# One ring of 22 places for all expert weights, loaded two slabs at a time over buffers that lie idle

## The chip, the core and the metric

The kernel runs on one core of a Trainium2 chip. The metric is the device time of one execution in microseconds (us), as the median of several runs; a profiled execution gives the trace. TensorE does the matmuls, VectorE (DVE in the rows) and ScalarE (ACT) the elementwise work, and SyncE (SP) does nothing but issue DMAs, which bring the weights from device memory into the on-chip memory. All engines run their own instruction streams and meet at semaphores.

## The reference

One inference step of a two-layer decoder for 288 tokens (256 of a prompt and 8 x 4 new ones), in fp32, width 1024. Each layer mixes three recurrent branches (retention, gated linear attention, RWKV-7) and then applies a feed-forward part. The change concerns the second layer, whose feed-forward part picks two of eight experts for each token:

```python
def swiglu(h, w1, w3, w2):
    return (jax.nn.silu(h @ w1) * (h @ w3)) @ w2

def moe_swiglu(h, router, w1, w3, w2):
    logits = (h @ router).astype(jnp.float32)
    top_v, top_i = lax.top_k(logits, TOP_K)
    probs = jax.nn.softmax(top_v, axis=-1)
    gate = jnp.sum(jax.nn.one_hot(top_i, N_EXPERTS, dtype=jnp.float32) * probs[..., None], axis=-2)
    out = jnp.zeros(h.shape, jnp.float32)
    for e in range(N_EXPERTS):
        out = out + gate[..., e:e + 1] * swiglu(h, w1[e], w3[e], w2[e]).astype(jnp.float32)
    return out.astype(h.dtype)
```

w1 and w3 of an expert are 1024 x 2816, w2 is 2816 x 1024; the three are 34.6 MB in fp32, for each of eight experts.

## The kernel before

The program runs through both layers in stages; in the second layer the mixing stage ends with a merging stage (`mix_out`: three pairs of gate slabs, four of the RWKV branch and four of the output projection, eleven "join pairs" in all), and then comes `experts`. Weights arrive as slabs of 128 x 1024 fp32 (512 KB) on a ring of eight places, `ring`, in the order in which TensorE uses them. SP issues one DMA for a slab as soon as the slab that held the place before is done, which it reads from one counter, `slab_done`.

In `experts` the tokens of an expert are gathered and the expert runs over at most `cap` of them. There are eight passes here, the experts in order of the number of their tokens: two passes at a capacity of 88, two at 80, two at 76 and the rest, two here, at 72. For each capacity there is one piece of code, and a loop runs it twice. A pass has

- an up part: 44 slabs of w1 and w3, one after the other by turns, each 16 matmul calls (8 blocks of rows by two halves of 64 columns), with ScalarE's silu and VectorE's product behind it;
- between: the matrix that scatters the results (`scatter_matrix`) and the gather for the next pass (`gather_tokens`);
- a down part: eight column blocks of w2, two at a time (`down`, 44 matmul calls each), then the results are added to the tokens (`add_up`, `to_tokens`).

TensorE's code for the up part is a loop (`pe.Fori`) of five turns over eight slabs and four slabs behind it, that of the down part a loop of four turns over two column blocks. The up slabs use the eight places of `ring`; the down weights come as 24 slabs (16 of 512 KB, 8 of 384 KB) on six places of their own over `proj`, an idle buffer. At the start of the first pass eight up and six down slabs have been asked for. SP's order in a pass is: six down slabs, up slabs 8 to 43, the first eight up slabs of the expert that follows, the other 18 down slabs. In the last pass the expert that follows is none, and its eight slabs are loaded and not used.

These lines of the profile belong to it: L302 matmuls of the earlier stages, L455 matmuls of an up slab, L2659 of a down slab, L2618 and L2624 the gather, L2646 the scatter matrix, L2670 and L2677 the additions, L2704 the sums of the closing norm; L442, L2524 and L2530 are SP's loads.

Of the kernel before, what the change touches and what calls it, by code (L numbers as in the profile page):

```python
# [22 lines left out]
D = 1024  # L23
# [4 lines left out]
T = NP + NS  # L28
# [26 lines left out]
RING = 8  # L55
SIDE_BEGUN = 6
# [39 lines left out]
FF_SLABS = UP_SLABS + DOWN_SLABS  # L96

# [124 lines left out]
def build(nc, xT_in, w_mix, w_lora, w_rank, w_gkup, vec_in, vecf_in, router_in, w_ff, s_ret, s_gla, s_rw,  # L222
# [133 lines left out]
    slab_done = nc.alloc_semaphore(name="slab_done")  # L356
    rank_in = [nc.alloc_semaphore(name=f"rank_in{s}") for s in range(2)]
# [1752 lines left out]
    def slab_width(j):  # L2110
        return 6 if j >= UP_SLABS and (j - UP_SLABS) % 3 == 2 else KT

# [12 lines left out]
    def mix_out(nc, block, sig, layer, delta, joined):  # L2125
# [32 lines left out]
        def _(sp):  # L2158
            load_group(sp, S_RW_OUT, 1)
            load_first_group(sp, S_OUT)  # L2160
            if dense:
                for j in range(FF_SLABS):
# [298 lines left out]
    def experts(nc, block, sig, layer, merge, rs):  # L2461
# [22 lines left out]
        down_ring = proj[:, :, :].rearrange("p n t -> p (n t)")[:, 0:6 * D].rearrange("p (s k n) -> p s k n", s=6, k=KT)  # L2484
        DRING = 6
        down_in = [sig(f"down_in{s}") for s in range(DRING)]
# [4 lines left out]
        FREED = 4, 5, 6, 7, 0, 1, 2, 3  # L2491
# [16 lines left out]
        def _(sp):  # L2508
            def freed_up(p, n):

                if n >= RING:
                    return count(p, FF_SLABS, FF0 + n - RING + 1)
                return count(p, FF_SLABS, FF0 - FF_SLABS + max(range(n, UP_SLABS, RING)) + 1)

            def load_up(p, e, n):
                load_ff_slab(sp, e, n, n % RING, freed_up(p, n))

            def load_down(p, e, d):
                if d >= DRING:
                    sp.wait_ge(slab_done, count(p, FF_SLABS, FF0 + UP_SLABS + d - DRING + 1))  # L2520
                else:
                    sp.wait_ge(slab_done, count(p, FF_SLABS, FF0 - DRING + d + 1))
                n = slab_width(UP_SLABS + d)
                sp.dma_start(down_ring[:, d % DRING, 0:n], w_ff[e, UP_SLABS + d, :, 0:n]).then_inc(down_in[d % DRING], 16)  # L2524

            def load_following(i, e, turn):
                for n in FREED:
                    sp.wait_ge(slab_done, freed_up((i, turn), n))
                    settle(sp)
                    sp.dma_start(ring[:, n], w_ff[e, n]).then_inc(slab_in[n], 16)  # L2530

            def expert_of(i):
                return sp.value_load(ctl[0:1, i], min_val=0, max_val=NE)
# [33 lines left out]
        def _(pe):  # L2567
# [111 lines left out]
            def expert(p, cap):  # L2679
# [634 lines left out]
```

## Time and profile before

| what | us |
| --- | --- |
| median of 3 runs | 2499.25 (2497.41 to 2500.42) |
| the profiled execution: its time | 2499.8 |
| the profiled execution: span of its trace | 2498.0 |
| TensorE matmuls busy | 2434.0 (97% of the span) |
| TensorE weight loads busy | 2026.7 (81%) |
| VectorE busy | 1287.7 (52%) |
| ScalarE busy | 606.7 (24%) |

The span goes from the first to the last instruction of the trace; 1.8 us of the execution lie outside it. The granted TensorE clock was 0.997 of full speed over the execution. An engine's busy time says nothing about what it waits for in a given stage: the matmul row is counted as busy from the start of a matmul to a modelled end, so a stream that waits a little at every slab still looks busy.

### The profile page before, as it was taken

To read this page: it belongs to the slowest core of one execution; us is meant where nothing else is said; L and a number is where in the kernel's file an instruction comes from. 1 tells how busy PE (TensorE), PEld (TensorE's weight loads), DVE (VectorE), ACT (ScalarE), POOL (GpSimd) and SP (SyncE) were. 2 spreads that over 40 slices of the span, in tenths; PEclk is the share of its full clock that TensorE was granted. 3 is DMA by queue.
4 is the path that set the end of the run, shared out by engine and by line. 5 is a ranking of instruction groups with operands and counts; after the bars stand their busy time and mean duration, and the time that the engine had idled before them with its cause. 6 is when DMAs were issued, how large, how long until landed. Compare 5 with 4: busy or idle time off the path is not lost. (4 is left out here: it accounts for less than half of the span.)

```text
span 2498.0 us, 104094 instructions
## 1 busy us (share of the span) xinstructions
PE 2434.0 (97%) x45930; PEld 2026.7 (81%) x45930; DVE 1287.7 (52%) x3333; ACT 606.7 (24%) x1798; POOL 0.2 (0%) x4
## 2 busy tenths in 40 slices
PE   9999999999999999999999999999999999999998
PEld 8987666666698999898766666669899989888887
DVE  7666666666686675756666566668311111111111
ACT  2233333433311100223332334331111111111111
POOL 0000000000000000000000000000000000000000
PEclk9999999999999999999999999999999999999999
DMA  6334432222243453423443222223799999999997
GB/s 250 112 137 162 148 137 88 83 84 80 92 153 128 153 179 127 142 106 139 164 161 127 85 77 84 84 105 145 297 356 398 380 376 409 396 379 402 395 390 308
DMA packets 146064, 500.46 MB, mean 200 GB/s; under 512 B 18784, under 2 KB 23520, under 8 KB 143360
## 3 DMA queue, kind: packets, MB, share of 16 engines
q1 hardware_dynamic: 145792, 496.44, 53.6%
q8 instruction: 219, 3.59, 0.6%
q14 instruction: 53, 0.43, 0.1%
HBM read 476.08 MB, written 20.29 MB: 199 GB/s over the span
## 5 line engine op out<-in xcount | busy, mean ns | idle before, releaser
L302 PE MATMUL psum<-hT,ring 128*64 128x144 f32 (+1 forms) x4568 | 457.1, 346 | 3.4 <-DVE hT L2422 1.7
L455 PE MATMUL psum<-work,ring 128*64 128x88 f32 (+3 forms) x11264 | 417.5, 232 | 15.4 <-DMA ring<-w_ff_dram 5.7
L455 PEld LDWEIGHTS psum<-work,ring 128*64 128x64 f32 x11264 | 399.2, 136 | 34.6 <-issue 29.6
L302 PEld LDWEIGHTS psum<-hT,ring 128*64 128x64 f32 x4568 | 291.8, 137 | 97.0 <-issue 11.7
L2958 DVE TENSOR_TENSOR work<-psum,work 128x88 f32<-128x88 f32 (+3 forms) x176 | 42.4, 241 | 361.8 <-PE psum L455 361.6
L2659 PE MATMUL psum<-work,proj 128*64 128x88 f32 (+3 forms) x5632 | 204.8, 232 | 6.8 <-issue 5.6
L2659 PEld LDWEIGHTS psum<-work,proj 128*64 128x64 f32 x5632 | 197.5, 136 | 14.0 <-issue 11.5
L1768 ACT ACTIVATE work<-psum 128x256 f32<-128x256 f32 (+4 forms) x320 | 103.9, 362 | 349.9 <-PE psum L1679 84.8
L302 PE MATMUL psum<-y_ret,work 128*64 128x144 f32 x2400 | 157.8, 288 | 0.8 <-DVE y_ret L532 0.8
L302 PE MATMUL psum<-work 128*64 128x144 f32 (+4 forms) x2096 | 154.1, 282 | 4.3 <-DVE work L1259 3.6
L302 PEld LDWEIGHTS psum<-y_ret,work 128*64 128x64 f32 x2400 | 150.2, 138 | 1.3 <-issue 1.3
L302 PEld LDWEIGHTS psum<-work 128*64 128x64 f32 (+2 forms) x2096 | 121.3, 136 | 30.7 <-issue 11.3
L2949 DVE TENSOR_TENSOR xT<-xT,psum 128x288 f32<-128x288 f32 x64 | 29.1, 454 | 220.6 <-PE psum L2670 219.6
L2743 ACT ACTIVATE work<-psum 128x88 f32<-128x88 f32 (+3 forms) x176 | 41.7, 237 | 376.7 <-PE psum L455 373.2
L302 PE MATMUL psum<-y_ret,ring 128*64 128x144 f32 (+1 forms) x1280 | 126.8, 332 | 2.5 <-ACT work L1768 2.5
L302 PEld LDWEIGHTS psum<-y_ret,ring 128*64 128x64 f32 x1280 | 79.5, 137 | 18.5 <-ACT work L1768 4.5
L324 PE MATMUL psum<-hT,ring 128*128 128x288 f32 x252 | 72.8, 408 | 0.0
L1564 PEld LDWEIGHTS psum<-work 64*64 64x64 f32 x1408 | 47.3, 134 | 29.4 <-issue 17.7
L547 DVE TENSOR_TENSOR y_gla<-psum,y_gla 128x288 f32<-128x288 f32 x72 | 33.0, 458 | 73.2 <-PE psum L302 72.6
L302 PE MATMUL psum<-hT,work 128*64 128x144 f32 x928 | 68.8, 287 | 0.0
L2747 ACT ACTIVATE work<-psum 128x88 f32<-128x88 f32 (+3 forms) x64 | 15.2, 237 | 218.3 <-PE psum L2659 218.3
L519 DVE TENSOR_TENSOR work<-ring 128x512 f32<-128x512 f32 (+1 forms) x90 | 54.7, 608 | 19.0 <-PE psum L302 19.0
(518 smaller groups left out, 3723.9 us busy)
## 6 DMA issues: line engine op xcount, KB each, us to landing
ring<-w_ff_dram SPq DMA_DIRECT2D x424, 512.0 KB, 7.6
ring<-w_mix_dram SPq DMA_DIRECT2D x256, 512.0 KB, 4.2
proj<-w_ff_dram SPq DMA_DIRECT2D x128, 512.0 KB, 5.5
proj<-w_ff_dram SPq DMA_DIRECT2D x64, 384.0 KB, 5.7
work<-s_gla_dram SPq DMA_DIRECT2D x8, 1024.0 KB, 5.0
gla_s_out<-work SPq DMA_DIRECT2D x8, 1024.0 KB, 4.7
work<-s_ret_dram SPq DMA_DIRECT2D x8, 512.0 KB, 5.6
ret_s_out<-work SPq DMA_DIRECT2D x8, 512.0 KB, 3.0
```

Of the source, the lines that this page charges most:

```text
L302: last = nc.tensor.matmul(out[64 * c:64 * c + 64], weights[:, 64 * c:64 * c + 64], x, start=start, stop=stop)
L324: mm = (in_halves if self.narrow else nc.tensor.matmul)(out, ring[:, s, k, :], rhs[:, k, :], start=(k == 0), stop=(k == KT - 1))
L455: mm = nc.tensor.matmul(out[64 * c:64 * c + 64], ring[:, s, k, 64 * c:64 * c + 64], rhs[:, k0 + k, :], start=(k0 + k == 0), stop=(k0 + k = ...
L519: op.tensor_tensor(s1, a21, a22, ALU.add).then_inc(sig("wsum"), 1)
L547: nc.vector.tensor_tensor(c[:, 1:3, :], two(LAST_TWO[side]), c[:, 5:7, :], ALU.add).then_inc(sig("outer"), 1)
L1564: last = mm(unit(half(W, r), c), half(AT, 1 - r)[:, c], half(X, 1 - r)[:, c], start=True, stop=True)
L1768: return nc.scalar.activation(out, in_, func, **kw)
L2659: last = mm(DOWN[m][64 * h:64 * h + 64, 0:cap], down_ring[:, d, k, 64 * h:64 * h + 64], hid[:, KT * c + k, 0:cap], start=(KT * c + k == 0) ...
L2743: ac(act1[:, f % 2, 0:cap], bank[2 * f % 4][:, 0:cap], ACT.Silu).then_inc(sig("w1_free"), 1)
L2747: ac(oT[:, m % 2, 0:cap], DOWN[m % 2][:, 0:cap], cp).then_inc(sig("oT"), 1)
L2949: tt(xT[:, k, :], xT[:, k, :], ADD[m % 2][:, 0:T], ALU.add).then_inc(sig("added"), 1)
L2958: tt(hid[:, f, 0:cap], bank[(2 * f + 1) % 4][:, 0:cap], act1[:, f % 2, 0:cap], ALU.mult).then_inc(sig("w3_free"), 1)
```

## The change

All 22 places for expert weights become one ring, `ex_slot`: two over `lora_w`, two over `hT`, two over `y_ret`, six over `proj`, the eight of `ring` and two over `merged`, all buffers that hold nothing at that time. The down weights are packed so that they fill 22 whole slabs; an expert is then 66 slabs, three times round the ring. One DMA brings two slabs (1 MB) into a pair of places, with one semaphore for a pair. The first 22 slabs are asked for during the merging stage, each pair when its buffer's last reader is done, and the load of eight slabs of a following expert goes away. Since place and part of the expert no longer repeat within a part, TensorE's code names each slab's place by itself: the two inner loops go, and the code of a pass stands in a row.

```diff
+EX_RING = 22
...
+EX_DOWN = D // 128 * FT // KT
+EX_SLABS = UP_SLABS + EX_DOWN
...
+    def slabs_in(buffer, n):
+
+        return buffer.rearrange("p a b -> p (a b)")[:, 0:n * D].rearrange("p (s k m) -> p s k m", s=n, k=KT)
+
+    EX_AT_LORA, EX_AT_HT, EX_AT_Y, EX_AT_PROJ, EX_AT_RING, EX_AT_MERGED = 0, 2, 4, 6, 12, 20
+    pair_in = {s: slab_in[s - EX_AT_RING] if EX_AT_RING <= s < EX_AT_MERGED else nc.alloc_semaphore(name=f"pair_in{s}")
+               for s in range(0, EX_RING, 2)}
+    ex_pair = [x[:, i:i + 2] for x, n in ((slabs_in(lora_w[:, :, :], 2), 2), (slabs_in(hT[:, :, :], 2), 2),
+                                          (slabs_in(y_ret[:, :, :], 2), 2), (slabs_in(proj[:, :, :], 6), 6),
+                                          (ring, RING), (slabs_in(merged[:, :, :], 2), 2)) for i in range(0, n, 2)]
+    ex_slot = [x[:, i] for x in ex_pair for i in range(2)]
+
+    def load_pair(sp, e, n):
+
+        s = n % EX_RING
+        sp.dma_start(ex_pair[s // 2], w_ff[e, n:n + 2].rearrange("s p k m -> p s k m")).then_inc(pair_in[s], 16)
...
+            def ahead(*slots):
+                for n in slots[::2]:
+                    load_pair(sp, 1, n)
+
...
             else:
-                for j in range(RING):
-                    load_ff_slab(sp, 1, j, j, FF0 + j - RING + 1)
+                for s in range(RING):
+                    sp.wait_ge(slab_done, slabs_before(layer, S_RW_OUT) + s + 1)
+                    sp.dma_start(ring[:, s], w_mix[layer, BASE[S_RW_OUT] + RING + s]).then_inc(slab_in[s], 16)
+                    if s == 3:
+                        sp.wait_ge(slab_done, join_done(0))
+                        ahead(*range(EX_AT_LORA, EX_AT_HT))
+                sp.wait_ge(slab_done, join_done(JOIN_GATES - 1))
+                ahead(*range(EX_AT_HT, EX_AT_PROJ))
+                load_first_group(sp, S_OUT)
+                sp.wait_ge(slab_done, join_done(OUT0 - 1))
+                ahead(*range(EX_AT_PROJ, EX_AT_RING))
+                for q in range(OUT0, JOIN_PAIRS):
+                    sp.wait_ge(slab_done, join_done(q))
+                    ahead(EX_AT_RING + 2 * (q - OUT0), EX_AT_RING + 2 * (q - OUT0) + 1)
+                ahead(*range(EX_AT_MERGED, EX_RING))
...
-            p = 0, 0
-            for d in range(DRING):
-                load_down(p, 1, d)
-            for n in range(RING, UP_SLABS):
-                load_up(p, 1, n)
-            rest = passes(sp)
-            load_following(0, expert_of(slice(0, 1)), 1)
-            for d in range(DRING, DOWN_SLABS):
-                load_down(p, 1, d)
...
+            def load(p, e, n):
+                sp.wait_ge(slab_done, count(p, EX_SLABS, FF0 + n - EX_RING + 2))
+                load_pair(sp, e, n)
+
+            for n in range(EX_RING, EX_SLABS, 2):
+                load((0, 0), 1, n)
+            sp.wait_ge(sig("ctl"), 1)
             after_first = sp.value_load(ctl[0:1, ENTRIES + 1:ENTRIES + 2], min_val=NE - 1, max_val=FIXED - 1 + MAXR)
             with sp.Fori(0, after_first) as i:
-                e = expert_of(bass.ds(i, 1))
-                following = expert_of(bass.ds(i + 1, 1))
-                p = i, 1
-                for d in range(DRING):
-                    load_down(p, e, d)
-                for n in range(RING, UP_SLABS):
-                    load_up(p, e, n)
-                load_following(i, following, 2)
-                for d in range(DRING, DOWN_SLABS):
-                    load_down(p, e, d)
+                e = sp.value_load(ctl[0:1, bass.ds(i, 1)], min_val=0, max_val=NE)
+                for n in range(0, EX_SLABS, 2):
+                    load((i, 1), e, n)
...
-            def up(p, cap, n, turn):
-
-                i, done = p
-                s = n % RING
-                per = len(range(s, UP_SLABS, RING))
-                fill = fills_before(layer, s) + fills(len(STREAM), s) + done * per + n // RING + 1
-                pe.wait_ge(slab_in[s], turn * 16 + (i * (per * 16) + fill * 16))
-                pe.wait_ge(sig("w3_free" if n % 2 else "w1_free"), turn * (RING // 2) + count(p, FT, n // 2 + 1))
+            def pair_here(p, n):
+
+                s = n % EX_RING
+                earlier = 0
+                if EX_AT_RING <= s < EX_AT_MERGED:
+                    earlier = fills_before(layer, s - EX_AT_RING) + fills(len(STREAM), s - EX_AT_RING)
+                pe.wait_ge(pair_in[s], count(p, EX_SLABS // EX_RING * 16, (earlier + n // EX_RING + 1) * 16))
+
+            def up(p, cap, n):
+
+                if n % 2 == 0:
+                    pair_here(p, n)
+                pe.wait_ge(sig("w3_free" if n % 2 else "w1_free"), count(p, FT, n // 2 + 1))
                 if n in (2, 3):
                     pe.wait_ge(sig("oT"), count(p, KT, n - 1))
-                narrow_products(pe, s, bank[n % 4][:, 0:cap], hg[:, :, 0:cap])
+                for k in range(KT):
+                    for h in range(2):
+                        last = mm(bank[n % 4][64 * h:64 * h + 64, 0:cap], ex_slot[n % EX_RING][:, k, 64 * h:64 * h + 64],
+                                  hg[:, k, 0:cap], start=(k == 0), stop=(k == KT - 1))
+                last.then_inc(slab_done, 1)
...
+            def down(p, cap, m):
+
+                pe.wait_ge(sig("oT"), count(p, KT, m + 1))
+                for f in range(FT):
+                    n, k = divmod(FT * m + f, KT)
+                    if k == 0 and n % 2 == 0:
+                        pair_here(p, UP_SLABS + n)
+                    for h in range(2):
+                        last = mm(DOWN[m % 2][64 * h:64 * h + 64, 0:cap],
+                                  ex_slot[(UP_SLABS + n) % EX_RING][:, k, 64 * h:64 * h + 64], hid[:, f, 0:cap],
+                                  start=(f == 0), stop=(f == FT - 1))
+                    if k == KT - 1:
+                        last.then_inc(slab_done, 1)
+                    elif f == FT - 1:
+                        last.then_inc(sig("down_ps"), 1)
...
-                with pe.Fori(0, UP_SLABS // RING) as g:
-                    for n in range(RING):
-                        up(p, cap, n, g)
-                for n in range(UP_SLABS // RING * RING, UP_SLABS):
-                    up(p, cap, n, 0)
+                for n in range(UP_SLABS):
+                    up(p, cap, n)
                 scatter_matrix(p)
                 pe.wait_ge(sig("otok"), count(p, KT, 2))
                 pe.wait_ge(sig("added"), count(p, KT, 2))
                 gather_tokens(count(p, 1, 2), cap)
                 pe.wait_ge(sig("w3_free"), count(p, FT, FT + 2))
-                settle(pe)
-                with pe.Fori(0, KT // 2) as t:
-                    for m in range(2):
-                        down(p, cap, t, m)
-                    for m in range(2):
-                        add_up(p, t, m)
-                    for m in range(2):
-                        to_tokens(p, t, m)
+                for m in range(0, KT, 2):
+                    down(p, cap, m)
+                    down(p, cap, m + 1)
+                    add_up(p, m)
+                    add_up(p, m + 1)
+                    to_tokens(p, m)
+                    to_tokens(p, m + 1)
...
             def take_down(p, cap, m):
-                act.wait_ge(slab_done, count(p, FF_SLABS, FF0 + UP_SLABS + 3 * m + 3))
+                if m % 4 == 3:
+                    act.wait_ge(slab_done, count(p, EX_SLABS, FF0 + UP_SLABS + 11 * (m // 4) + 11))
+                else:
+                    act.wait_ge(sig("down_ps"), count(p, 6, m // 4 * 3 + m % 4 + 1))
```

SP in the merging stage of the second layer, before: the ring's own loads and eight expert slabs, then, behind the branch into `experts`, the first down slabs and the rest of the first expert's up slabs (`w_mix_dram` holds the layer's own weights, `w_ff_dram` the experts').

```order
L2157 UNCONDITIONAL_BRANCH
L415 DMA ring<-w_mix_dram 128x1024 x8
L423 DMA ring<-w_mix_dram 128x1024 x8
L442 DMA ring<-w_ff_dram 128x1024 x8
L2507 UNCONDITIONAL_BRANCH
L2524 DMA proj<-w_ff_dram 128x1024 x2
L2524 DMA proj<-w_ff_dram 128x768
L2524 DMA proj<-w_ff_dram 128x1024 x2
L2524 DMA proj<-w_ff_dram 128x768
L442 DMA ring<-w_ff_dram 128x1024 x36
```

The same place on SP in the changed kernel.

```order
L2175 UNCONDITIONAL_BRANCH
L2196 DMA ring<-w_mix_dram 128x1024 x4
L376 DMA lora_w<-w_ff_dram 128x2x1024
L2196 DMA ring<-w_mix_dram 128x1024 x4
L376 DMA hT<-w_ff_dram 128x2x1024
L376 DMA y_ret<-w_ff_dram 128x2x1024
L444 DMA ring<-w_mix_dram 128x1024 x8
L376 DMA proj<-w_ff_dram 128x2x1024 x3
L376 DMA ring<-w_ff_dram 128x2x1024 x4
L376 DMA merged<-w_ff_dram 128x2x1024
L2538 UNCONDITIONAL_BRANCH
```

Eleven pair loads now stand in the merging stage, three of them ahead of the output projection's eight slabs; the ring loads keep their order.

TensorE at the end of the up part and in the whole down part of the capacity 88, before: the last four up slabs, the scatter matrix, the gather and the body of the down loop, which ends with its branch back (a row's x44 counts the matmul calls of one column block).

```order
L455 MATMUL psum<-work,ring 64x88 x32
L2636 REGISTER_ALU
L455 MATMUL psum<-work,ring 64x88 x32
L2644 REGISTER_ALU
L2646 MATMUL psum<-table,work 88x128 x2
...
L2694 UNCONDITIONAL_BRANCH
L2694 ISA
L2655 ISA
L2659 MATMUL psum<-work,proj 64x88 x44
L2652 REGISTER_ALU
L2659 MATMUL psum<-work,proj 64x88 x44
...
L2694 COMPARE_AND_BRANCH
```

The down part of the same capacity in the changed kernel, its first four of eight column blocks (176 calls of `down`).

```order
L2657 MATMUL psum<-work,lora_w 64x88 x32
L2657 MATMUL psum<-work,hT 64x88 x32
L2657 MATMUL psum<-work,y_ret 64x88 x24
L2672 MATMUL psum<-work 64x288 x4
L2678 REGISTER_ALU
L2679 MATMUL psum<-table,work 88x128
L2678 REGISTER_ALU
L2679 MATMUL psum<-table,work 88x128
L2657 MATMUL psum<-work,y_ret 64x88 x8
L2657 MATMUL psum<-work,proj 64x88 x80
L2672 MATMUL psum<-work 64x288 x4
```

The order of the matmuls is the same, but the branch back is gone and each column block has calls of its own: 704 calls instead of 192 in the up part's code, 352 instead of 88 in the down part's, beside the 43 calls between the parts and six for each turn of the down loop (in the code once before, four times now).

## Rows read from the trace of the kernel before

**Rows 1.** The page's span and TensorE's line: busy us, share, matmul records.
```profile
span 2498.0 us, 104094 instructions
...
PE 2434.0 (97%) x45930; PEld 2026.7 (81%) x45930; DVE 1287.7 (52%) x3333; ACT 606.7 (24%) x1798; POOL 0.2 (0%) x4
```

**Rows 2.** Windows: merging stage, fourth and seventh pass; last columns clock, DMA share, GB/s.
```profile
1676.00:1771.00 95.00, 91.79 (x1384) 84.16 (x1384) 69.69 (x166) 17.11 (x37) 0.00 (x0) 1.00 0.45 165
...
2046.00:2133.00 87.00, 85.82 (x2237) 80.24 (x2238) 13.14 (x42) 11.86 (x42) 0.00 (x0) 1.00 1.02 399
...
2310.00:2398.00 88.00, 82.73 (x2235) 74.64 (x2233) 12.33 (x41) 10.93 (x39) 0.00 (x0) 1.00 1.00 387
```

**Rows 3.** Chain that ended last: start us, length us, what, count of matmul records.
```profile
1865.13 54.39 PE psum L455 x1408
...
1931.22 6.92 PE psum L2659 x176
1939.46 6.92 PE psum L2659 x176
...
1956.25 8.65 PE psum L455 x242
...
2046.10 24.77 PE psum L455 x704
...
2117.55 6.24 PE psum L2659 x176
2125.11 6.24 PE psum L2659 x176
...
2222.43 17.20 PE psum L455 x512
...
2309.86 11.41 PE psum L455 x352
...
2331.82 8.59 DMA ring<-w_ff_dram
2342.06 8.59 DMA ring<-w_ff_dram
...
2469.29 5.76 PE psum L2659 x176
2476.38 5.69 PE psum L2659 x176
2484.84 4.11 PE psum L2704 x16
```

**Rows 4.** Timeline of TensorE: first up slabs of the first pass.
```profile
1771.16 6.37 PE L455 MATMUL psum<-work,ring 128*64 128x88 f32 x160 [0.34 <-issue]
```

**Rows 5.** DMA queues, 1676 to 1771 us: instruction queue's packets, MB, share.
```profile
q8 instruction: 11, 0.18, 0.8%
```

**Rows 6.** DMA queues, 2133 to 2222 us (first pass at 76): instruction queue.
```profile
q8 instruction: 5, 0.08, 0.3%
```

**Rows 7.** DMA queues, 2046 to 2133 us (second pass at 80): the only queue.
```profile
q1 hardware_dynamic: 9828, 34.72, 101.6%
```

**Rows 8.** Timeline of TensorE, first pass at 76; in brackets idle time before.
```profile
2190.26 0.49 PE L2624 MATMUL psum<-work 128*64 128x76 f32 x9 [0.69 <-issue]
2190.99 4.04 PE L2659 MATMUL psum<-work,proj 128*64 128x76 f32 x116 [0.24 <-issue]
2196.42 2.20 PE L2659 MATMUL psum<-work,proj 128*64 128x76 f32 x60 [1.39 <-issue]
```

**Rows 9.** DMA queues, 2193.5 to 2195.5 us: instruction queue.
```profile
q8 instruction: 1, 0.02, 3.3%
```

**Rows 10.** Timeline of TensorE, first pass at 72.
```profile
2365.46 1.60 PE L2624 MATMUL psum<-work 128*64 128x72 f32 x45 [0.27 <-issue]
2366.97 2.78 PE L2659 MATMUL psum<-work,proj 128*64 128x72 f32 x81
2371.64 3.22 PE L2659 MATMUL psum<-work,proj 128*64 128x72 f32 x95 [1.89 <-issue]
```

More of the change, by code:

```diff
@@ L2108, in _ @@
             norm(KT - 1)
-    def slab_width(j):
-        return 6 if j >= UP_SLABS and (j - UP_SLABS) % 3 == 2 else KT
     def down_pairs(j):
@@ L2508, in _ @@
         def _(sp):
[L2509 to L2533, printed above, removed]
-            p = 0, 0
-            for d in range(DRING):
-                load_down(p, 1, d)
-            for n in range(RING, UP_SLABS):
-                load_up(p, 1, n)
@@ L2559, in _ @@
             sp.wait_ge(sig("stored"), 4 * 16)
-            for s in range(RING):
-                per = len(range(s, UP_SLABS, RING))
-                fill = fills_before(layer, s) + fills(len(STREAM), s) + FIXED * per + 1
-                sp.wait_ge(slab_in[s], rest * (per * 16) + fill * 16)
-                settle(sp)
         @block.tensor
@@ L2647, in scatter_matrix @@
                 last.then_inc(sig("scatter_ps"), 1)
-            def down(p, cap, t, m):
-                i, done = p
-                pe.wait_ge(sig("oT"), t * 2 + count(p, KT, m + 1))
-                for c in range(3):
-                    d = 3 * m + c
-                    pe.wait_ge(down_in[d], t * 16 + (i * 64 + (done * 64 + 16)))
-                    n = 6 if c == 2 else KT
-                    for k in range(n):
-                        for h in range(2):
-                            last = mm(DOWN[m][64 * h:64 * h + 64, 0:cap], down_ring[:, d, k, 64 * h:64 * h + 64],
-                                      hid[:, KT * c + k, 0:cap], start=(KT * c + k == 0), stop=(KT * c + k == FT - 1))
-                    last.then_inc(slab_done, 1)
@@ L2665, in add_up @@
+            def add_up(p, m):
                 if m == 0:
                     pe.wait_ge(sig("hg"), count(p, 1, 2))
-                pe.wait_ge(sig("otok"), t * 2 + count(p, KT, m + 1))
-                pe.wait_ge(sig("added"), t * 2 + count(p, KT, m + 1))
+                pe.wait_ge(sig("otok"), count(p, KT, m + 1))
+                pe.wait_ge(sig("added"), count(p, KT, m + 1))
                 for h in range(2):
-                    last = mm(ADD[m][64 * h:64 * h + 64, 0:T], otok[0:CAP, m, 64 * h:64 * h + 64], scatter[0:CAP, :], start=True,
-                              stop=True)
+                    last = mm(ADD[m % 2][64 * h:64 * h + 64, 0:T], otok[0:CAP, m % 2, 64 * h:64 * h + 64], scatter[0:CAP, :],
+                              start=True, stop=True)
@@ L2672, in add_up, with to_tokens @@
                 last.then_inc(sig("sc_ps"), 1)
-            def to_tokens(p, t, m):
-                pe.wait_ge(sig("oT"), t * 2 + count(p, KT, m + 3))
-                nc.tensor.transpose(OTOK[m][0:CAP, 0:128], oT[:, m, :], ident).then_inc(sig("otok_ps"), 1)
+            def to_tokens(p, m):
+                pe.wait_ge(sig("oT"), count(p, KT, m + 3))
+                nc.tensor.transpose(OTOK[m % 2][0:CAP, 0:128], oT[:, m % 2, :], ident).then_inc(sig("otok_ps"), 1)
             def expert(p, cap):
@@ L3269 @@
             continue
-        for c in range(3):
-            n = 6 if c == 2 else 8
-            w_ff[e, UP_SLABS + c::3, :, 0:n] = s2[:, :, 8 * c:8 * c + n]
+        w_ff[e, UP_SLABS:EX_SLABS] = s2.transpose(0, 2, 1, 3).reshape(EX_DOWN, KT, 128, 128).transpose(0, 2, 1, 3)
     vec = np.concatenate([feat(a[k]) for k in ("norm_mix", "norm_ffn", "gla_gk_bias", "gla_norm_w")]
```

14 lines of the change are left out of this document (4 added, 10 removed).

## The prediction

> **What bounds the kernel now.** I read the share of time by engine first [rows 1]: TensorE is busy 97% of the 2498.0 us, so whatever lengthens or shortens its stream shows in the end. The change touches the last part, eight expert passes (the rate moved there is near what the queue can do all the time), so I read that stretch by windows [rows 2] and then the chain that ended last inside it [rows 3]. The first pass begins at 1771.16 [rows 4], the last ends at about 2484 (2476.38 + 5.69 + 1.3 for the last additions, and the closing sums start at 2484.84) [rows 3]. That is 713 us for eight passes, and 14 us follow.
>
> Two rates compete there. TensorE's own: one up slab takes 54.39/44 = 1.236 us at a capacity of 88, 24.77/22 = 1.126 at 80, 17.20/16 = 1.075 at 76 and 11.41/11 = 1.037 at 72; a turn of the down loop takes 8.24 us at 88 (start to start, 1931.22 to 1939.46), 7.56 at 80 and 7.09 at 72 [rows 3], and I put 7.35 at 76, between its neighbours. The pass that starts at 1865.13 and ends at 1956.25 is TensorE's from end to end: 91.1 us = 54.4 for up, 33.0 for down, 3.7 for the scatter matrix and the gather between. With the same 3.7 the other capacities need 83.4, 80.4 and 77.7 us. All eight: 2 x 332.6 = 665 us.
>
> The queue's: the chain repeats itself every 10.24 us (2331.82 to 2342.06), with two runs of a load and one of TensorE, for 8 slabs [rows 3]. A slab of 512 KB therefore lands every 1.28 us, and 66 slabs' worth of bytes need 84.5 us. So passes of capacity 88 are bound by TensorE, and the later ones by the queue: they last 87 to 88 us [rows 2] where TensorE needs 78 to 83. The eight passes hold 713 - 665 = 48 us in which TensorE waits, nearly all for weights.
>
> **The change part by part.**
>
> *A longer ring and an earlier start.* Now 14 slabs are there when the first pass begins, afterwards 22; the eight slabs of a further expert that are loaded in the last pass and never used go away. From the second slab of the first pass to the end 264 - 11 = 253 pairs have to land, 253 x 2.56 = 648 us, against 665 us of TensorE's own work. With 22 slabs (28 us) of lead the queue may fall behind by 84.5 - 77.7 = 7 us in each of the last two passes, 4 in the two before them and 1 in the two before those without being missed: 24 us in all. Taken alone this part removes almost all of the 48 us; I leave 4 us for the places where pairs come free too late, and the first pass's own gaps. That is -44 us.
>
> *Loads ahead in the merging stage.* Eight slabs more, 4 MB, in a stage where the queue's engines are busy 0.45 of the time at 165 GB/s [rows 2]: 55% of 95 us is 52 us of room for 8 x 1.28 = 10 us of load. On SP the first pair stands behind a wait that the next ring load has anyway, and the next two (5.1 us) stand ahead of the output projection's slabs, whose places come free one 8 us pair later at the earliest. I cost it at nothing; without that cover it is at most those 5.1 us.
>
> *Transfers of two slabs.* Same bytes, same 4 KB rows, half as many issues. SP is not the limit. Nothing; but the first slab of a pair now waits for both, at most 1.28 us once, when the ring is empty.
>
> *TensorE's code.* This is the part that costs. Before, a pass runs 128 matmul calls in a loop, then 107, then 94 in a second loop; after, all 1,123 calls of a pass stand one behind the other. A call leaves two weight loads and two matmuls in the trace (one each for a transpose), so a pass grows from about 1,350 instructions to 4,550, with its waits and register steps. The instruction queue shows how code arrives. In the merging stage, which has no loops, 11 fetches of 16 KB stand beside 1,384 matmuls and 1,384 weight loads [rows 5, 2]: 2,768/11 = 252 instructions to a fetch, so 64 bytes each and 256 to a block. The first pass of a capacity fetches 5 blocks [rows 6], which is its 1,350 instructions; the second pass of the capacity 80 fetches none at all (the queue's line stands alone there) [rows 7]. So a body of 5.3 blocks is held; one of 17.8 blocks is nowhere in this trace.
>
> What a block costs when the queue is full can be read in the first passes. At 76, TensorE starts at 2190.26 after a stop, runs 9 + 116 matmuls and as many loads (250 instructions, with the waits one block), and stops again until 2196.42, with no releaser [rows 8]; the fetch of that next block begins between 2193.5 and 2195.5 [rows 9]. At 72 the same from 2365.46 over 45 + 81 matmuls to 2371.64 [rows 10]. From a block's first instruction to the next block's: 6.16 and 6.18 us, of which 1.39 and 1.89 us is standstill. So the next block is asked for only about when its predecessor begins, and among full data queues it takes 6.2 us to be usable. Up code runs a block (3.92 slabs) in 4.07 to 4.85 us.
>
> The Trainium skill says the same of the mechanism (Runtime: NRT & Kernel Launch, section "Instruction fetch mechanics"): blocks of 16 KiB fetched in sequence, a TensorE store of 128 KiB or 2,048 instructions, and a stall after a taken branch whose target is not there. By it the new body would be fetched again in every pass; no run here shows a body of that size yet. It also says that a block's crossing is mostly hidden, and in rows 8 and 10 it is not.
>
> I take the new body as fetched again in every pass, since it is 3.4 times the largest that the trace shows held and is in kind like the merging stage's straight code. Then the wait regulates itself. Where TensorE outruns the queue, loads pile up, a block takes up to 6.2 us and TensorE falls below the queue's pace (5.02 us for a block's 3.92 slabs); then the pile shrinks and blocks come sooner. So I put the up part of each pass at the queue's pace, 44 x 1.28 = 56.3 us, at all four capacities, and the lead of 22 slabs buys nothing there. In the down part TensorE is slower than the queue by itself (7.09 to 8.24 us for 5.5 slabs, which land in 7.04), so blocks come soon. The 44 up slabs take 44/3.92 = 11.2 of the 17.8 blocks; to each of the other 6.6 I give 0.3 us, between nothing and the 1.89 us above, nearer the short stops (0.24 to 0.69) [rows 8].
>
> Passes: 56.3 + 3.7 + four turns of down, 93.0, 90.2, 89.4 and 88.4 us, twice: 722. Stops in down: 8 x 6.6 x 0.3 = 16. Four passes begin with a jump back to code that is 17 blocks away; bounds are nothing and 6.2 us, I take 4 because the queue is emptier there: 16. 1771 + 722 + 16 + 16 = 2525, + 14 = 2539 us of span, + 1.8 us that lie outside it (2499.8 against 2498.0), = 2541; the median of the runs lies 0.5 us below the profiled one, so 2540.
>
> **The rivals.**
> *The fetches hide.* If blocks are asked for early enough, or overtake the data, the first part alone counts: 2499 - 44 = 2455. For it: in the straight code of the merging stage TensorE is busy 91.79 of 95 us [rows 2]. Against: a block lasts 95/11 = 8.6 us there and the queue is half empty, while the full queue gave 6.2 us [rows 8, 10]. It decides if a block is usable within 4.1 us. It is the case for which the Trainium skill's "mostly hidden" (the section named above) stands.
> *The body is held after all.* Then only the four first passes pay: 361 + 8 + 333 = 702, 1771 + 702 + 16 = 2489, with queues full again after each quick pass 2480 to 2500. For it: rows 7. Against: the size.
> *A block always takes 6.2 us,* however empty the queue. Then 17.8 x 6.17 = 110 us for a pass, 8 x 110 + 16 = 896, 1771 + 896 + 16 = 2683. Against: a fetch waits for something, and the queue will be less full. [...]
>
> **How the numbers follow.** My forecast (2505 to 2580) 0.60; fetches hidden (2445 to 2480) 0.17; held, or a mild form of the forecast (2480 to 2505) 0.15; always dear (over 2580) 0.08. Below 0.2% (5 us) a difference can hardly be told from no change. Faster: 0.17 and half of the third, 0.25; within 0.2%: 0.06; slower: 0.69. The range from 2470 to 2580 leaves out the lower 25 of the hidden case's 35 us (0.12) and the dear case (0.08). The forecast's own range is 2505 to 2580.
>
> **What would show it.** Right: some 18 fetches of 16 KB in every pass, second ones too; standstills of 0.5 to 2 us on TensorE without a releaser, one to a block, in the up part; up parts of 55 to 58 us at all capacities; few waits for weights; a queue that is busy about 0.9 of the time; a stop of some us where the second pass of a capacity begins. Wrong: passes of 78 to 84 us, no fetches in second passes, or TensorE waiting for weights. The forecast falls if a block comes within 4.1 us under load, or if the code is held.

## The result, and the profile after

The changed kernel takes 2604.21 us (median of 4 runs, 2603.28 to 2606.95) against 2499.32 for the kernel before: a ratio of 1.0422, with a 95% interval of 1.0407 to 1.0436. That is 105 us more, where 41 more were forecast, and it lies above the range. The profiled execution took 2603.47 us.

The page's lines for the span, TensorE and the instruction queue, of the changed kernel.

```profile
span 2601.7 us, 102379 instructions
...
PE 2437.2 (94%) x45930; PEld 2039.8 (78%) x45930; DVE 1287.7 (49%) x3333; ACT 607.9 (23%) x1798; POOL 0.2 (0%) x4
...
q8 instruction: 346, 5.67, 0.9%
```

TensorE's busy time is 3.2 us above that of [rows 1], so nearly all of the 103.7 us between the two spans is idle time. The windows say where: they are the merging stage, the first and second passes at 80 and the first at 72 (the last columns are granted clock, DMA share, GB/s).

```profile
1676.00:1771.00 95.00, 91.97 (x1388) 84.28 (x1384) 69.73 (x164) 17.15 (x37) 0.00 (x0) 1.00 0.58 212
...
1974.50:2077.50 103.00, 85.56 (x2236) 80.15 (x2235) 13.38 (x43) 13.51 (x44) 0.00 (x0) 1.00 0.95 353
2077.50:2177.20 99.70, 87.07 (x2235) 81.62 (x2235) 12.88 (x41) 10.06 (x38) 0.00 (x0) 0.98 0.91 335
...
2381.70:2488.70 107.00, 82.12 (x2235) 76.82 (x2235) 12.72 (x42) 12.88 (x42) 0.00 (x0) 0.96 0.92 340
```

Against [rows 2] the merging stage has not moved, though it carries 212 GB/s instead of 165. A second pass at 80 is 99.7 us instead of 87, the first at 72 is 107 instead of 88, and the DMA engines, full before, now have some time left (shares of 0.91 to 0.95). The releasers of TensorE's idle time from the first pass to the last (1771 to 2588; us in total, times, longest):

```profile
PE psum L2637 <- issue: 106.9, 66, 5.9
PE psum L2657 <- issue: 13.9, 19, 2.0
PE psum L2637 <- DVE work L2959: 1.4, 1, 1.4
```

L2637 is now an up slab's matmul and L2657 a down slab's. No wait for a DMA stands in the answer: the weights are always there, and TensorE waits for nothing that the profile shows. What it waits for is seen in the timeline of the second pass at 80, its first half (in brackets the idle time before a group):

```profile
2077.55 3.84 PE L2637 MATMUL psum<-work,lora_w 128*64 128x80 f32 x64 [5.19 <-issue]
2081.22 2.39 PE L2637 MATMUL psum<-work,hT 128*64 128x80 f32 x64
...
2090.83 2.57 PE L2637 MATMUL psum<-work,proj 128*64 128x80 f32 x66 [0.60 <-issue]
2093.21 2.27 PE L2637 MATMUL psum<-work,ring 128*64 128x80 f32 x60
2096.16 4.61 PE L2637 MATMUL psum<-work,ring 128*64 128x80 f32 x127 [0.68 <-issue]
2102.31 2.64 PE L2637 MATMUL psum<-work,ring 128*64 128x80 f32 x69 [1.54 <-issue]
```

From 2090.83 to 2096.16 run 66 + 60 matmuls, from 2096.16 to 2102.31 another 127: with as many weight loads that is one block of 256 instructions each, in 5.33 and 6.15 us, and a standstill behind each. A block's matmuls alone take 3.92 x 1.126 = 4.41 us at this capacity. The packets of the instruction queue tie the standstills to the fetches: of the 90 that are longer than 0.2 us in the eight passes, 89 end 1.1 to 2.0 us (median 1.4) after a fetch of 16 KB has landed (worked out from the trace's packet times). And where [rows 7] had no fetch at all, the same pass now has these queues:

```profile
q1 hardware_dynamic: 8576, 33.09, 90.1%
q8 instruction: 18, 0.29, 1.1%
```

Eighteen fetches of 16 KB, which is the whole body of a pass. All eight passes have 18 or 19, first and second alike, and the median time from one fetch to the next lies between 5.5 and 5.8 us in each of them.

### The profile page after: what moved, and what is told of

Read it like the earlier page. It is cut to its first block and busy times, and to the rows that moved or that the text cites. A ratio compares the mean times of both kernels' runs of the same rounds, so it can differ in the third digit from the quotient of the medians.

```text
span 2601.7 us, 102379 instructions
## 1 busy us (share of the span) xinstructions
PE 2437.2 (94%) x45930; PEld 2039.8 (78%) x45930; DVE 1287.7 (49%) x3333; ACT 607.9 (23%) x1798; POOL 0.2 (0%) x4
## 5 line engine op out<-in xcount | busy, mean ns | idle before, releaser
L305 PEld LDWEIGHTS psum<-hT,ring 128*64 128x64 f32 x4568 | 293.3, 137 | 95.8 <-issue 11.7
L2637 PE MATMUL psum<-work,ring 128*64 128x88 f32 (+3 forms) x4096 | 153.4, 234 | 37.8 <-issue 37.7
L2637 PEld LDWEIGHTS psum<-work,ring 128*64 128x64 f32 x4096 | 148.0, 138 | 41.7 <-issue 41.7
L2741 ACT ACTIVATE work<-psum 128x88 f32<-128x88 f32 (+3 forms) x176 | 41.9, 238 | 469.3 <-PE psum L2637 465.7
L2637 PE MATMUL psum<-work,proj 128*64 128x88 f32 (+3 forms) x3072 | 113.5, 231 | 18.3 <-issue 18.3
L2637 PEld LDWEIGHTS psum<-work,proj 128*64 128x64 f32 x3072 | 109.2, 136 | 21.1 <-issue 21.1
L2657 PE MATMUL psum<-work,ring 128*64 128x88 f32 (+3 forms) x2048 | 75.2, 231 | 4.5 <-issue 4.5
L2657 PEld LDWEIGHTS psum<-work,ring 128*64 128x64 f32 x2048 | 72.3, 136 | 6.8 <-issue 6.8
L2637 PE MATMUL psum<-work,lora_w 128*64 128x88 f32 (+3 forms) x1024 | 46.4, 254 | 28.2 <-issue 28.2
```

Source lines behind the costliest of these rows:

```text
L305: last = nc.tensor.matmul(out[64 * c:64 * c + 64], weights[:, 64 * c:64 * c + 64], x, start=start, stop=stop)
L2637: last = mm(bank[n % 4][64 * h:64 * h + 64, 0:cap], ex_slot[n % EX_RING][:, k, 64 * h:64 * h + 64], hg[:, k, 0:cap], start=(k == 0), stop= ...
L2657: last = mm(DOWN[m % 2][64 * h:64 * h + 64, 0:cap], ex_slot[(UP_SLABS + n) % EX_RING][:, k, 64 * h:64 * h + 64], hid[:, f, 0:cap], start=( ...
L2741: ac(act1[:, f % 2, 0:cap], bank[2 * f % 4][:, 0:cap], ACT.Silu).then_inc(sig("w1_free"), 1)
```

## The experiments

The table gives the length of each pass, from its first up matmul to the next pass's (worked out from the traces; the last one ends at the last additions behind it), and the fetches of the instruction queue in it.

| kernel | 88 | 88 | 80 | 80 | 76 | 76 | 72 | 72 | sum | fetches |
| --- | --- | --- | --- | --- | --- | --- | --- | --- | --- | --- |
| TensorE's own time, from the prediction | 91.1 | 91.1 | 83.4 | 83.4 | 80.4 | 80.4 | 77.7 | 77.7 | 665 | |
| before | 94.0 | 91.1 | 89.8 | 86.8 | 89.5 | 87.4 | 88.6 | 85.2 | 712 | 5 first, 0 or 1 second |
| after | 103.7 | 99.7 | 103.0 | 99.7 | 104.7 | 99.9 | 107.0 | 99.2 | 817 | 18 to 19 |
| 1 old ring, straight code | 103.4 | 105.2 | 102.5 | 102.1 | 108.2 | 100.9 | 107.6 | 98.4 | 828 | 18 to 20 |
| 3 no loads after the first expert | 102.1 | 93.9 | 85.8 | 83.9 | 81.7 | 79.3 | 78.0 | 79.9 | 685 | 18 to 19 |
| 5 up part looped | 98.2 | 94.8 | 101.8 | 95.5 | 98.7 | 93.5 | 99.2 | 86.1 | 768 | 11 to 15 |
| 6 loads for six of eleven pairs | 103.7 | 94.1 | 91.5 | 89.3 | 86.3 | 81.4 | 90.4 | 89.7 | 726 | 18 to 19 |
| 7 twelve up places, looped | 101.7 | 96.9 | 98.6 | 95.5 | 95.8 | 91.2 | 95.4 | 85.9 | 761 | 7 to 10 |
| 9 fourteen up places, looped | 99.7 | 96.7 | 91.7 | 91.1 | 89.4 | 91.0 | 91.4 | 78.1 | 729 | 6 to 8 first, 0 or 1 second |

**1. The old rings with the code in a row.** Only the loops of the kernel before are written out; places, loads and their order stay.

```diff
-                with pe.Fori(0, UP_SLABS // RING) as g:
-                    for n in range(RING):
-                        up(p, cap, n, g)
-                for n in range(UP_SLABS // RING * RING, UP_SLABS):
+                for n in range(UP_SLABS):
                     up(p, cap, n, 0)
...
-                with pe.Fori(0, KT // 2) as t:
+                for t in range(KT // 2):
```

> The kernel before with its rings and its slab-wise loads, only TensorE's two inner loops written out in a row. Theory F (code fetches behind any stream of loads set the pace, about 5.7 us for a block of 256 instructions): 18 to 19 fetches in every pass, 2580 to 2610 us. Theory P (the fetch waits behind transfers, and transfers of 1 MB made it longer): blocks come sooner behind 512 KB loads, 2530 to 2570. Theory R (the new ring and its transfers cost the time, not the code): 2495 to 2510.

Measured: 2619.29 us (before on the same chip 2497.98), ratio 1.0492 (1.0475 to 1.051), 9 us above Theory F's range. TensorE's longest waits between 1771 and 2588:

```profile
PE psum L455 <- issue: 108.1, 70, 7.1
PE psum L2659 <- issue: 20.8, 24, 1.9
```

The code alone costs 121 us, more than the whole change, with the same kind of wait at the same places. The ring is not the cause; the changed kernel is 0.7% faster than this one (1.0422 against 1.0492), some 17 us. No wait for a DMA stands in this answer either: at the pace that the code allows, the old rings bring the weights in time. So the 17 us are not saved waits for weights. The waits for code are some 11 us shorter in after; why they are, and what the rest is, was not tried.

**2. The new ring, one slab to a transfer.**

```diff
-        sp.dma_start(ex_pair[s // 2], w_ff[e, n:n + 2].rearrange("s p k m -> p s k m")).then_inc(pair_in[s], 16)
+        for c in range(2):
+            sp.dma_start(ex_slot[s + c], w_ff[e, n + c]).then_inc(pair_in[s], 16)
...
```

> The changed kernel with one DMA of 512 KB for each slab instead of one of 1 MB for two; ring, places, order and code stay. F: unchanged within 10 us, 2595 to 2612. P: the median time between fetches falls from 5.7 to about 5 us and the time to 2530 to 2570.

Measured: 2602.33 us, ratio 1.0417 (1.0399 to 1.0434), the same as after. The size of a transfer changes neither the time nor, to speak of, the time from fetch to fetch (5.4 to 6.1 us). That larger transfers hold a fetch up longer does not show at these two sizes.

**3. No loads after the first expert.**

```diff
-            with sp.Fori(0, after_first) as i:
-                e = sp.value_load(ctl[0:1, bass.ds(i, 1)], min_val=0, max_val=NE)
-                for n in range(0, EX_SLABS, 2):
-                    load((i, 1), e, n)
...
```

> The changed kernel without the expert loads of the second to eighth pass; those passes work on the weights that already lie in the ring, so the outputs are not the reference's. F and P: without loads a block arrives within 4 us, so stops stay only where the code jumps back; passes of 91, 83, 83, 80, 80, 78, 78 us after the first, 2470 to 2490 in all. If a fetch is slow by itself, whatever the loads: still 18 stops a pass and 2570 to 2605.

Measured: 2469.71 us, ratio 0.9886 (0.9869 to 0.9902). The first pass at 80 in the windows, and in the timeline the second one's start:

```profile
1967.00:2053.00 86.00, 82.52 (x2227) 78.79 (x2225) 13.08 (x41) 12.03 (x42) 0.00 (x0) 0.99 0.02 4
```

```profile
2051.38 4.08 PE L2633 MATMUL psum<-work,lora_w 128*64 128x80 f32 x64 [3.48 <-issue]
```

The code is the same and is fetched again just as often, but with the data queue empty (share 0.02) the stops inside a pass are all but gone: from the second pass on each pass is within 3 us of TensorE's own time. So a block of code comes within 4.0 us when nothing else moves (the fetch period at 72, where TensorE needs 4.07 for it), and what costs is the fetch behind data, not the fetch. The jump back stays: TensorE stands still for 3.48 us even here, and for 2.8 to 3.5 at the four jumps of this kernel.

**4. No jump back.** For three capacities the two passes are written one behind the other, so that only the last capacity still jumps.

```diff
-                with pe.Fori(0, n) as i:
+                for i in range(n):
                     expert((i, before_it), cap)
```

> The changed kernel with the code of both passes of the capacities 88, 80 and 76 written one behind the other on TensorE, so that three of four jumps back fall away. If a jump back costs two blocks in a row and a spell at half clock behind it, 8 to 10 us each: 2574 to 2582. If it costs no more than one more block's stop, 1.4 us each: 2598 to 2602.

Measured: 2586.85 us, ratio 1.0353 (1.0336 to 1.037). Three jumps cost 2604.21 - 2586.85 = 17.4 us, 5.8 each, between the two prices that were expected. The stops between blocks stay (91.5 us in 74 waits at the up slabs).

**5. The up part in two turns over the ring**, so that 22 slabs of up code are in the program instead of 44.

```diff
-                for n in range(UP_SLABS):
-                    up(p, cap, n)
+                with pe.Fori(0, UP_SLABS // EX_RING) as g:
+                    for n in range(EX_RING):
+                        up(p, cap, n, g)
...
```

> The changed kernel with the up part as a loop of two turns over the 22 places, so its second turn runs code that was just fetched; ScalarE, VectorE and TensorE name the PSUM banks by place instead of by slab for it. A pass is then some 3,370 instructions or 13.2 blocks instead of 17.8. If the price is per block fetched: 13 to 14 fetches in a pass and a quarter of the lost 150 us less, 2560 to 2575. If code of more than one pass's held size gains nothing from a loop inside it: 2595 to 2608.

Measured: 2555.51 us, ratio 1.023 (1.0213 to 1.0247). The loop saves 49 us of the 105, and the fetches fall to 11 to 15 in a pass, about the 12 blocks that are left of the body, fetched once each. They still come in every pass.

**6. Loads for six of the eleven pairs of places** after the first expert.

```diff
                 for n in range(0, EX_SLABS, 2):
-                    load((i, 1), e, n)
+                    if n % EX_RING % 4 == 0:
+                        load((i, 1), e, n)
...
```

> The changed kernel where after the first pass only 6 of the 11 pairs of places are loaded again; the other five keep old weights, so the outputs are not the reference's. The data queue is then busy about half of the time. If a block's wait shrinks with the load, as the prediction had it: median between fetches near 4.5 to 5 us, 2490 to 2530. If any stream of loads keeps it near 5.7 us: 2570 to 2600.

Measured: 2514.66 us, ratio 1.0057 (1.004 to 1.0075). The windows of the second pass at 80, the first at 76 and the first at 72:

```profile
2059.00:2148.00 89.00, 85.65 (x2236) 81.38 (x2234) 12.86 (x41) 10.04 (x39) 0.00 (x0) 0.97 0.59 204
2148.00:2234.00 86.00, 79.94 (x2236) 75.93 (x2235) 13.13 (x43) 13.37 (x44) 0.00 (x0) 1.00 0.69 235
...
2315.70:2406.00 90.30, 77.67 (x2235) 72.62 (x2235) 12.73 (x42) 12.85 (x42) 0.00 (x0) 0.99 0.64 223
```

From the second pass on, with DMA shares of 0.57 to 0.69 (0.43 in the last pass), fetches come 4.3 to 5.0 us apart, and 4.7 in the first pass at 72, where TensorE, which needs 4.07, stops at block after block. In the passes at 88 to 76 TensorE itself needs 4.2 to 4.85 us for a block, so these bound the wait only from above. The stops at the up slabs fall from 106.9 us to 42.5 in all. So the wait does fall with the load, which the prediction's "regulates itself" needs; it falls too slowly for the pace that I gave it.

**7. Twelve up places with looped code.** The kernel before, with `lora_w` and `y_ret` as four more up places and no loads for an expert that does not follow; the loading engine's loop is turned, so that a turn starts with the next expert's up slabs.

```diff
+    UP_RING = 12
+    up_slot = [ring[:, s] for s in range(RING)] + [two_slabs(x)[:, s] for x in (lora_w[:, :, :], y_ret[:, :, :]) for s in range(2)]
...
-                with pe.Fori(0, UP_SLABS // RING) as g:
-                    for n in range(RING):
+                with pe.Fori(0, UP_SLABS // UP_RING) as g:
+                    for n in range(UP_RING):
                         up(p, cap, n, g)
...
```

> The kernel before with its loops, an up ring of 12 places instead of 8 (four over idle buffers) and no loads for an expert that does not follow; down ring and slab-wise loads stay. If the loops' code is held and the lead is what the passes lack: 44 us of waits shrink by the 10 us of unused loads, 5 us of lead and some of the rest, 2465 to 2485, faster than both kernels. If the six places of the down ring set the pace: 2488 to 2495.

Measured: 2546.41 us, ratio 1.019 (1.017 to 1.0209), slower, which neither side expected. Twelve slabs in the loop and eight behind it make 320 up calls instead of 192, and the pass, some 1,870 instructions or 7.3 blocks, is no longer held: 7 to 10 fetches in each pass, second ones too.

**8. Eight up places, without the unused loads**: kernel 7 with `UP_RING = RING`.

> The kernel before with SP's loop turned round, so that the eight slabs of an expert that does not follow are never loaded; TensorE's code and the rings stay. The body of some 1,360 instructions stays held, no fetches in second passes; the last pass's down weights come up to 10 us sooner: 2487 to 2494, faster than before. If the unused loads hid behind the down part: 2497 to 2501.

Measured: 2512.77 us, ratio 1.0056 (1.0043 to 1.0069). The code is held again (0 fetches in second passes), and yet it is 13 us slower than before. That was a miss; kernel 11 takes the two edits apart. Kernels 7 and 9 have the same turned loop, so part of what they lose, 13 us if it costs as much there, is not due to their places.

**9. Fourteen up places**: kernel 7 with `hT` as two more places. Fourteen slabs go three times into 42, so only two stand behind the loop: 256 up calls.

> The same with 14 up places (six over idle buffers): TensorE's up loop has three turns over 14 slabs and two behind it, PSUM banks named by place; the body of a pass grows to some 1,620 instructions, 6.3 blocks. The held size lies between 5.7 blocks (the loop of the run with the looped up part) and 7.3 (the run with 12 places). If 6.3 is held: no fetches in second passes and 20 slabs of lead, 2455 to 2475. If not: 7 to 8 fetches in every pass and 2520 to 2545.

Measured: 2517.1 us, ratio 1.0075 (1.0063 to 1.0087), between the two sides. The body (some 1,620 instructions, 6.3 blocks) is held: six to eight fetches in first passes, none or one in second ones. But TensorE now waits for down weights; in the second pass at 76, first in the timeline, then in the chain of work:

```profile
2304.43 5.82 PE L2659 MATMUL psum<-work,proj 128*64 128x76 f32 x88 [6.77 <-DMA proj<-w_ff_dram]
```

```profile
2291.77 12.61 DMA proj<-w_ff_dram
```

The load of a down slab takes 12.61 us from issue to landing. The next expert's fourteen up slabs were asked for ahead of it, eight of them in the 6.6 us before, which by 1.28 us a slab are some 10 us of load. That this order is what makes it late was argued here; kernel 10 changes the order.

**10. The same, up and down slabs asked for in turn.** Also with the last pass apart, as in kernel 11.

```diff
+                for t, share in enumerate((4, 2, 2, 2, 2, 2)):
+                    done = sum((4, 2, 2, 2, 2, 2)[:t])
+                    for n in ups[done:done + share]:
+                        load_up(q, f, n)
+                    for d in range(DRING + 3 * t, DRING + 3 * t + 3):
+                        load_down(p, e, d)
...
```

> The kernel with fourteen places for up slabs (twelve looped places of up code, down code in its loop of 16 turns), whose long stops stood at the start of the down part because all fourteen up slabs of the next expert were asked for ahead of this expert's down slabs 6 to 23. Here the two are asked for in turn: 4, 2, 2, 2, 2, 2 up slabs, each lot followed by three down slabs; the next expert's control entry is read once a pass, as in the kernel before, and the last expert's pass is written apart, so that nothing is loaded that isn't used. Theory D (those stops are down slabs that come late behind the up slabs): the stops of 5 to 7 us at the start of the down part go, in each of the later seven passes one, so 2517 minus some 35 to 40 us: 2475 to 2485. Theory Q (fourteen slabs ahead only move the same bytes, and the data queue sets the pass: 38 slabs of 512 KB need about 85 us whatever their order): the stops turn up elsewhere, and it comes out at 2505 to 2520.

Measured: 2558.02 us (before 2498.53), ratio 1.024 (1.0222 to 1.0258): 41 us worse than kernel 9, which neither side expected. (The code has fourteen looped up places and four turns of the down loop, and theory Q's 85 us are those of all 66 slabs' worth of bytes of a pass, not of 38.) The gather behind the up part and the first down slabs in the second pass at 80, and for kernel 10 the down part after them, in windows of kernel 10 and then of kernel 9 (DMA share is the last column but one):

```profile
2134.50:2140.50 6.00, 6.00 (x177) 5.92 (x178) 1.30 (x4) 0.01 (x1) 0.00 (x0) 1.00 0.12 36
2140.50:2172.00 31.50, 23.70 (x558) 20.40 (x552) 2.73 (x6) 3.28 (x14) 0.00 (x0) 1.00 1.01 396
```

```profile
2108.00:2114.00 6.00, 5.58 (x151) 5.15 (x149) 1.54 (x5) 1.08 (x1) 0.00 (x0) 1.00 1.02 417
```

After four up slabs SP stands at the wait for a down place, which comes free only when the down part has begun, with ten further up slabs behind it whose places are coming free. The queue lies all but idle for 6 us, and then is full through the down part, where TensorE waits for down weights 29 times (60.1 us between 1771 and 2540, the longest 3.5; 23.5 in 11 waits in kernel 9, the longest 6.8). A wait in an in-order stream held back loads that had nothing to do with it. One thing stays unexplained: TensorE's code is that of kernel 9, yet the second pass at 88 fetched seven blocks again here, and one there.

**11. The kernel before with the last pass apart**, so that only the unused loads go.

> The kernel before with nothing changed but that the last expert's pass on the loading engine is written apart, so that the eight up slabs and six down slabs that no expert uses are not loaded; the order of the loads and the one read of the control entry per pass stay as before. Theory U (the unused loads cost the last pass and the combining stage behind it something, and the slower result of the kernel with the turned loop came from its two reads of control entries between up slabs): 2488 to 2495. Theory N (nothing waits for the unused loads, the engines have work beside them): 2497 to 2502, and then the turned loop's loss of 13 us is all due to where its reads stand.

Measured: 2497.85 us, ratio 0.9999 (0.999 to 1.0008). The unused loads cost nothing. What kernel 8 lost therefore comes from its turned loop, whose start, with two control entries to read, stands between the up slabs; that this reading is the price was not tried by itself. No version beat the kernel before.

## Why the prediction was wrong

The direction and the mechanism were right: the straight code is fetched again in every pass, TensorE stops for it at most of the blocks of the up part (62 stops beside those at the jumps, for some 90 blocks), and that outweighs the longer ring. The step that failed is a mis-sized term, "the wait regulates itself", with the up part "at the queue's pace".

**The up part's pace.** I reasoned that loads pile up only while TensorE outruns the queue, so a block would settle at 5.02 us, the queue's time for its 3.92 slabs. That takes it for granted that a block is quick as soon as the queue is a little less than full. Measured, fetches come 4.0 us apart or less with no loads (kernel 3), 4.7 at a DMA share of 0.64 (kernel 6, first pass at 72) and 5.5 to 5.8 at about 0.9 (after). So the up parts took 60.7 to 66.7 us from their first to their last matmul, longest at 72, and not 56.3 at all capacities.

The packet times of after show the wait itself. In the 63 blocks of 115 to 130 matmuls that lie between two stops, the fetch of the next block begins 3.5 us after the block does, takes 1.0, and TensorE goes on 1.4 after it has landed: 6.0 in all (medians). With the data queue idle the same took 2.7 us in one case, behind a jump of kernel 3: TensorE begins at 2374.29, the fetch runs from 2374.64 to 2375.73, and TensorE, which has stopped, goes on at 2376.95. So what the loads add is the time ahead of the fetch; when the fetch was asked for, the trace does not show.

Why the wait stays that long with the queue a little under full is open. A pace of 5.7 us makes a share of 5.02/5.7 = 0.88, but this follows from the bytes alone and explains nothing. The mean share does not fix the wait either: in kernel 6 the up part of the second pass at 76 ran with fetches 4.1 us apart at a share of 0.69, as fast as TensorE needs them there, and that of the first pass at 72 with 4.7 at 0.70. The rival "always 6.2 us" erred the other way.

**The sum, term by term.** Over TensorE's own 665 us the prediction had 57 (up parts) + 16 (down parts) + 16 (jumps) = 89 us; measured are 817 - 665 = 152. The up parts took 504.7 us in all where TensorE needs 393.6, so they lost 111 us, not 57: 99 in stops (each counted from where the next matmul would have begun at TensorE's own pace) and the rest at the lower clock, below. The jumps lost 23, not 16: their stops are 4.89 + 5.19 + 5.85 + 5.93 us in the rows, which count from a modelled end some 0.17 us behind the next group's start where nothing waits (2077.55 + 3.84 against 2081.22). My 4 us took the queue to be emptier there, which it is, but an empty queue still leaves 2.8 to 3.5 us (kernel 3), and beside the loads one costs 5.8 (kernel 4). The remaining 18 are the down parts and what lies between, near the forecast 16.

**What I had not on the list: the clock.** Before, the granted clock in these passes is 1.00 [rows 2]. After, the trace's clock records have nine spells at the lower level (1.2 GHz) between 1771 and 2588, 44 us together, each at or behind a stop of 2.0 to 5.9 us; seven other stops of 2.0 to 2.7 us had none. The windows of the second pass at 76, right after its jump back and then later, and the timeline of the same slabs:

```profile
2281.87:2286.00 4.13, 4.13 (x76) 4.13 (x77) 0.00 (x0) 0.24 (x1) 0.00 (x0) 0.58 0.04 12
2286.10:2289.40 3.30, 3.30 (x106) 3.30 (x104) 0.45 (x2) 0.47 (x2) 0.00 (x0) 1.00 0.64 218
```

```profile
2281.87 3.96 PE L2637 MATMUL psum<-work,lora_w 128*64 128x76 f32 x64 [5.85 <-issue]
...
2287.77 2.27 PE L2637 MATMUL psum<-work,y_ret 128*64 128x76 f32 x64
```

Two slabs take 3.96 us instead of 2.27 right after the stop. By the starts of the matmuls, those of the up parts that ran in the nine spells took 15 us longer than at TensorE's own pace, stops left out, which is what the 99 us of stops leave of the 111, within 3 us. So the clock is a smaller part; the stops are the main one.

**The rest.** That the lead of 22 slabs "buys nothing" in the up part came out: no wait for weights is left, but with code in a row none is left with the old rings either (kernel 1), and the 17 us between kernel 1 and after are not explained. The merging stage hides the early loads (the first pass starts at 1771.1, as before), and two-slab transfers cost nothing (kernel 2). The rival "fetches hide" holds only without loads, and there not at the jumps (kernel 3). By the sentence of the Trainium skill behind it (Runtime: NRT & Kernel Launch, section "Instruction fetch mechanics") a block's crossing is mostly hidden; the runs disagree wherever the data queue is busy, by 121 us in kernel 1. The rival "held after all" fell with the 18 fetches of second passes. The Trainium skill (the same section) gives TensorE a store of 2,048 instructions, which is eight blocks. Here 6.3 blocks were held (kernel 9) and 7.3 were not (kernel 7); as 7.3 blocks that begin inside a block lie in eight or nine, the runs fit that store as well as a smaller one.

## What to carry to other kernels

Count a loop body in blocks of 256 instructions before writing it out: where the weights fill the DMA queues, code that is no longer held costs a stop at most blocks, here 121 us (kernel 1), and the 48 us that TensorE waited before, nearly all of it for weights by the prediction's account, could not have paid for that. A ring whose length does not divide the work costs code, so choose a length that leaves few slabs behind the loop. And when a wait falls with the load that causes it, don't take it to vanish as soon as the queue is a little less than full; measure it at a part load first.

## What the runs showed of the hardware

- From one 16 KB fetch of code to the next: at most 4.0 us with an idle data queue (kernel 3, at 72), 4.7 at a DMA share of 0.64 (kernel 6, first pass at 72), 5.5 to 5.8 at about 0.9 (after); whether loads come as 512 KB or 1 MB made no difference (2602.33 and 2604.21 us).
- Where a block lies between two stops, the next fetch begins 3.5 us after the block, takes 1.0, and TensorE goes on 1.4 later (after, medians of 63 blocks); with an idle data queue the fetch began after 0.35 us and TensorE went on 2.7 us after its start behind the jump (kernel 3, one case).
- A pass of 6.3 blocks was held and ran its second time with no fetch or one (kernel 9), with one exception of seven fetches in kernel 10; a pass of 7.3 blocks was fetched again, 7 to 10 blocks each time (kernel 7).
- A jump back to code that is not held costs 2.8 to 3.5 us of standstill without loads (kernel 3), 4.89 to 5.93 with them (after), and 5.8 us of the kernel's time (kernel 4).
- At or behind nine standstills of 2.0 to 5.9 us the granted clock was at 1.2 GHz for a stretch, and not behind seven others of 2.0 to 2.7 us (after): 3.96 us for two slabs that take 2.27 at 2.4 GHz.
